# TensorE's order in the attention steps: value products ahead of the turns

## The reference

```
s = (q @ k.T) * scale + mask
p = softmax(s)                   # over the keys
o = p @ v
```

## Time and profile before

| what | value |
|---|---|
| median of the runs | 2418.43 us |
| the profiled execution | 2416.78 us, of which the span is 2415.5 us |
| TensorE (PE) busy | 2334.5 us, 97% of the span |
| weight loads (PEld) busy | 1908.5 us, 79% |
| VectorE (DVE) busy | 1863.8 us, 77% |
| ScalarE (ACT) busy | 1154.1 us, 48% |
| mean granted TensorE clock | 0.995 |
| HBM | 177 GB/s over the span |

### The profile page before, as it was taken

One profiled execution on the slowest core, in us unless ns is written; L12 is line 12 of the kernel. 1 busy time (PEld: TensorE's weight loads), 2 busy tenths in 40 slices (PEclk: granted clock), 3 DMA queues, 4 the chain that ended last, 5 costly groups with the idle time before them and its releaser, 6 DMA issues. The chain is left out here.

```text
span 2415.5 us, 37030 instructions
## 1 busy us (share of the span) xinstructions
PE 2334.5 (97%) x11673; PEld 1908.5 (79%) x11673; DVE 1863.8 (77%) x4229; ACT 1154.1 (48%) x1992; POOL 177.8 (7%) x204
## 2 busy tenths in 40 slices
PE   7989999999999999999999999999999999999997
PEld 5766467868787888888888867787788888888886
DVE  6677776778997788888888855699877777777776
ACT  5674247332485544444444436317744444444443
POOL 1000000001470000000000000026400000000000
PEclk9999999999999999999999999999999999999999
DMA  6524641572215677776677741411255555555553
GB/s 257 194 104 149 240 161 36 195 268 78 79 36 173 235 260 250 253 257 251 252 260 252 252 171 70 148 53 45 88 198 189 189 191 188 191 188 192 188 190 137
DMA packets 144609, 429.26 MB, mean 178 GB/s; under 512 B 15230, under 2 KB 21374, under 8 KB 144510
## 3 DMA queue, kind: packets, MB, share of 16 engines
q1 hardware_dynamic: 144510, 428.08, 50.5%
HBM read 426.99 MB, written 1.05 MB: 177 GB/s over the span
## 5 line engine op out<-in xcount | busy, mean ns | idle before, releaser
L3484 PE MATMUL bank<-v_parts,weighted_high 128*128 128x512 f32 x1952 | 528.4, 392 | 0.5 <-DVE weighted_low L3627 0.5
L3470 PE MATMUL bank<-h_t_parts,u_t_high 128*128 128x512 f32 x1824 | 450.5, 389 | 0.0
L3484 PEld LDWEIGHTS bank<-v_parts,weighted_high 128*128 128x128 f32 x1952 | 351.1, 189 | 65.3 <-issue 2.6
L3470 PEld LDWEIGHTS bank<-h_t_parts,u_t_high 128*128 128x128 f32 x1824 | 342.4, 188 | 71.0
L3548 ACT ACTIVATE u_t_high<-u_ring 128x1024 fp32r<-128x1024 f32 x228 | 242.0, 1061 | 181.3 <-DMA u_ring<-in_peer_u 179.1
L3567 ACT ACTIVATE activated<-activated 128x256 f32<-128x256 f32 x228 | 95.4, 418 | 475.9 <-DVE activated L3615 475.9
L3602 DVE TENSOR_TENSOR u_t_low<-u_ring,u_t_high 128x1024 fp32r<-128x1024 f32 x228 | 278.6, 1222 | 31.8 <-ACT u_t_high L3548 23.8
L3484 PE MATMUL bank<-v_parts,weighted_low 128*128 128x512 f32 x976 | 301.5, 390 | 0.0
L3609 DVE TENSOR_TENSOR v_parts<-v_ring,v_parts 128x1024 fp32r<-128x1024 f32 x242 | 294.0, 1215 | 3.3 <-ACT v_parts L3555 3.3
L3555 ACT ACTIVATE v_parts<-v_ring 128x1024 fp32r<-128x1024 f32 x242 | 255.1, 1054 | 48.2 <-PE bank L3484 46.8
L3473 PEld LDWEIGHTS bank<-h_t_parts,u_t_low 128*128 128x128 f32 x1824 | 248.8, 190 | 17.8
(11 more groups left out here) (601 smaller groups left out, 3460.3 us busy)
## 6 DMA issues: line engine op xcount, KB each, us to landing
v_ring<-in_peer_v SPq DMA_DIRECT2D x244, 512.0 KB, 3.4
u_ring<-in_peer_u SPq DMA_DIRECT2D x228, 512.0 KB, 4.6
panel<-in_l_w_in SPq DMA_DIRECT2D x15, 2048.0 KB, 8.4
late_tiles<-in_ada_w SPq DMA_DIRECT2D x54, 512.0 KB, 4.4
mod_ring<-in_ada_w SPq DMA_DIRECT2D x42, 512.0 KB, 4.5
panel<-in_peer_w_q SPq DMA_DIRECT2D x8, 2048.0 KB, 7.7
panel<-in_l_w_out SPq DMA_DIRECT2D x4, 2560.0 KB, 9.0
early_u<-in_peer_u SPq DMA_DIRECT2D x20, 512.0 KB, 3.4
```

The lines of the kernel that those rows point to most:

```text
L3470: nc.tensor.matmul(banks[2 + k][:, :], UTH[:, k, j, :], H2[:, j, :, :].rearrange("p a s -> p (a s)"), start=(j == 0), stop=False, skip_gro ...
L3484: last = nc.tensor.matmul(banks[4 + 2 * t + half][:, :], w[:, t * P:(t + 1) * P], v[k][:, half * 512:(half + 1) * 512], start=opens and n ...
```

## The change

Within TensorE's iteration `s`, the block that issues the values of step `s - VALUE` is moved ahead of the block that issues the turns of step `s - TURN`. The scores stay first. The waits of each block move with it, and nothing else is changed: same instructions, same banks, same semaphores and counts. ScalarE's and VectorE's programs are the same.

```diff
@@ -1027,6 +1027,17 @@
                                                     start=True, stop=True)
                         last.then_inc(scored, 1)
+                    if s >= VALUE:
+                        j, w = s - VALUE, steps[s - VALUE]
+                        pe.wait_ge(pt_ready, j + 1)
+                        if j >= 2:
+                            pe.wait_ge(out_done, outs_by[j - 2])
+                        tiles = w["nk"] // P
+                        for x in range(rows(w)):
+                            for k in range(tiles):
+                                last = nc.tensor.matmul(banks[4 + j % 2][:, x * HD:(x + 1) * HD], pt_sb[j % 2][:, x * tiles + k, :],
+                                                        w["v"][x][k], start=(k == 0), stop=(k == tiles - 1))
+                        last.then_inc(pv_done, 1)
                     if 0 <= s - TURN < N:
                         j, w = s - TURN, steps[s - TURN]
                         if w["lam"] is not None:
@@ -1042,17 +1053,6 @@
                                                            ident[:, :])
                         last.then_inc(turned, 1)
-                    if s >= VALUE:
-                        j, w = s - VALUE, steps[s - VALUE]
-                        ...
-                        last.then_inc(pv_done, 1)
```

## The result

| | before | after |
|---|---|---|
| median of 6 runs each | 2418.39 us (2416.42 to 2418.95) | 2430.08 us (2428.84 to 2430.99) |
| profiled execution, span | 2416.78, 2415.5 us | 2429.66, 2428.4 us |
| TensorE busy | 2334.5 us | 2337.3 us |
| mean granted clock | 0.995 | 0.993 |

The ratio is 1.005 (95%: 1.004 to 1.006): 11.7 us slower by the medians, against 2431.4 us predicted. In the kernel after, the values stand at L1038 and the turns at L1053.

What follows compares the result with a forecast made beforehand. TensorE's stream, its order fixed by hand in the three attention calls, was taken as the bound. Calls 3.1 + 3.7 + 3.5 and clock 2.7 make 13.0 us on the median 2418.43: 2431.4 us, range 2427.5 to 2435.0.

Steps and rivals of the forecast that it cites:

- The mechanism: All three calls: values first make TensorE stand at the later of two releases, the earlier one's work queued behind.
- Third call: Third call: 14 steady steps lose 0.13 us each, 1.8 us, and the end 1.3 us; sum 3.1 us.
- Second call: Second call: six pairs lose 2.0 us, the first eight steps 1.0, the end 0.7; sum 3.7 us.
- First call: First call: seven pairs lose 0.9 us, steps 16 to 18 0.5, the end 2.1; sum 3.5 us.
- The clock: Behind the third call: granted clock falls as behind the second, from longer idle time at the end; 2.7 us.
- The two terms taken at 0: Low stretches: the first call's vanishes or grows (−1.7 to +1.4 us), the second's shifts (−0.5 to +0.5).
- The span of 8.5 to 12.5: All three calls: range in us claimed for the loss by the order alone, without the clock.
- The first call's own stretch: Behind the first call in before: low clock for 3.4 us, 1.7 us lost at half rate, which could vanish.
- (a): Rival: the clock does not fall behind the third call; 10.3 us of loss alone, 2428.7 us; chance 0.25.
- (b): Rival: faster, values fill the turns' waits in first and second calls; up to 10.3 us gained, 2408; chance 0.03.
- (c): Rival: waits absorbed in slack or later DMA waits; within 4 us, 2419; chance 0.09, including losses under 4.8 us.
- (d): Rival: clock falls inside a call, in every second pair of the first; 7.4 us more, 2438.8 us; chance 0.08.

Runs made afterwards that it cites:

- e5: Against after: values one step further back (VALUE 4 in the first call, 3 in the others), wider row statistics, values still ahead of turns; 2410.36 us, ratio 0.9967.
- e1: Against before: values ahead of the turns in the third call only; 2421.90 us, ratio 1.0018.
- e7: Against after: matmuls whose results nobody uses put into TensorE's idle time at each call's end; 2428.38 us, ratio 1.0042.
- e4: Against before: values ahead of the turns in all calls while scores are issued, old order in the drain; 2423.92 us, ratio 1.0024.
- e2: Against before: values ahead of the turns in the first call only; 2421.45 us, ratio 1.0016.
- e3: Against before: values ahead of the turns in the second call only; 2421.45 us, ratio 1.0013.
- e8: Against e5: VectorE's outputs an iteration earlier, at the end of its iteration behind second minimum and joining; 2405.72 us, ratio 0.9946.
- e6: Against before: values one step further back (VALUE 4, 3, 3), wider row statistics, turns still ahead of values; 2416.97 us, ratio 0.9993.

## Why the prediction was right, and where it was not

- **The mechanism** (TensorE stands at the later of two releases) held in all three calls: in the third each group of values waits for ScalarE's copy, in the second both of a pair's do once the sparse steps run evenly, in the first one of a pair's two; no turn waits in the steady steps. e5 confirms it from the other side: with the release a step earlier, the loss turns into a gain.
- **Third call**: 3.1 predicted, 3.24 measured. Two steps took 4.65 (4.66 predicted), the last values started 5.61 after the last scores (5.56 by the prediction's sum of releases: 3.38 + 0.83 + 0.72 + 0.63). e1 reproduces the call alone.
- **Second call**: 3.7 predicted, 4.07 measured. The pair grew by 0.26 us instead of 0.33, and the last values started 5.02 after the last scores, as said; but the low clock began before they were done (1.78 us of loads). e7, at full clock, has 3.23. So the order's part was put 0.5 too high and the place at which the clock fell was missed.
- **First call**: 3.5 predicted, 3.07 measured. The pair grew by 0.06 us, not 0.13: the values' loads hand over to the turn after 0.39 us (159.47 to 159.86) where they handed over to the scores after 0.44, and the turn takes 0.11: steady steps 0.82 (e4) instead of 1.4; the end 2.25 against 2.1.
- **The clock, the step that failed**: "I take it that the clock falls there as behind the second call", 2.7 us. It fell, but for 3.4 us and not 6.8, and cost 1.0 (e7: 5.96 to 4.95). The reason given, the longer idle time at the new end, is not shown: e2 and e3 have the fall behind the old end, so that it may have come by chance. The two terms taken at 0 were not 0: behind the first call the stretch doubled and cost 1.0 more than before, and the second call's began inside the call, for 0.8. Low stretches in other stages (123, 642, 1650 us) came and went as well, net 0.4 with what else differs, which no term covered. Without these 0.8 in the second call the order cost 9.6 against 10.3 predicted, and the clock and the rest some 3.2 against 2.7. That the sum of 13.0 meets the 12.9 between the profiled executions is therefore in part luck; against the medians (11.7) it is 1.3 high.
- **The bounds.** The span of 8.5 to 12.5 for the order is not what the prediction's own bounds add up to, 6.7 to 13.0; the 10.4 lie in both. The first call's own stretch was priced at up to 1.7 us; by e1 it cost nothing.
- **Rivals.** (a) did not come true in the profiled execution (0.57 in the window at 1514 us), though its time, 2428.7, is as near the median as the forecast's, and the other five executions have no profile. (b) does not happen in this change, as the copies end behind the turns' release; it does in e5 and e8. (c) is ruled out by e1 to e3. (d) did not occur between the pairs of the kernel after, only in the last values of its second call, and did once in the first call of e2, for 1.7 us. The Trainium skill's section on the clock going up and down from small idle times between matmul groups ("TensorE: Matmul & The Clock Gate", "A second HAM failure mode: psum-queue depth-cycling") agrees with that one row (0.51 at 150.5 us) and not with after's three calls, where TensorE idles 12.9 of 42.9 us in the first at 1.00.

What stays open: why the stretches at 123, 642 and 1650 us, and those behind the first and third calls, come and go with a change far from them. Each moves the time by 0 to 2.2 us, as much as a term of the sum.

## What to carry to other kernels

In a pipeline whose order is written by hand, compare for each group the time at which it is released with the time of the group that shall stand behind it: the one released later goes last. To gain from another order, first move the later group's release (one step more between producer and consumer, if the buffers allow it), and then look for the next wait, here the one on a freed bank. Price the rounds at the end of a loop separately: with 16 to 20 steps they made half of the loss. And where the clock moves between executions, ask for its price in more than one profile, also of kernels that leave the place as it was.

## What the runs showed of the hardware

- With some matmuls into an unused bank in each drain the granted clock stayed at 1.00 behind all three calls. The three low stretches that this removed (6.8, 6.8 and 3.4 us long) had cost 0.9 us each at VectorE's later instructions. Behind the first call TensorE's first matmul on `src_high` comes 2.9 us sooner, and TensorE then waits 1.70 us for VectorE (e7, 199.76).
- One with nothing changed nearby, 3.4 us long, cost 1.7 us at once (647.4, e7 against after). TensorE had waited 3.22 us for VectorE just before it in e7, and at the same place in after, where the clock stayed at 1.00.
- Behind an end of the third call with the same groups and waits, the clock stayed at 1.00 in one execution (before) and fell for 3.4 us in another (e3, 1510.5), for 1.7 us of time.
- The order of the same three groups changes TensorE's time where nothing waits: 2.14 us a step with values before turns (e5), 2.20 with turns before values (before, e6), in the third call. Why is not shown.
- TensorE's loads start 0.05 us behind the end of the copy that releases them (first call after: copy until 159.42, loads at 159.47).
